# Transposes placed between the products of the next half unit, and the retention's projection moved ahead of the attention gate

## What is computed

```
h = rmsnorm(x, norm1_g) * (1.0 + scale1) + shift1
q_r, k_r, v_r, g_r, q_d, k_d, v_d, gates = split_projection(h @ w_in)
gate_r, gate_d = jnp.split(jax.nn.sigmoid(gates + b_gate), 2, axis=-1)
...
branch_r = (jax.nn.silu(g_r) * y_r) @ w_ret_out        # y_r: normalised output of the retention
branch_d = o_d @ w_diff_out                            # o_d: normalised output of the attention
mix = (gate_r * branch_r + gate_d * branch_d) @ w_o
x = x + gate1 * mix
h2 = rmsnorm(x, norm2_g) * (1.0 + scale2) + shift2
ffn = (jax.nn.silu(h2 @ w_ffn_gate) * (h2 @ w_ffn_up)) @ w_ffn_down
x = x + gate2 * ffn
```

## Time and profile before

| what | value |
|---|---|
| median of three runs | 1375.28 us (1375.09 to 1375.91) |
| the profiled execution | 1375.61 us, of which the span of instructions is 1373.9 us |
| PE busy | 1307.0 us |
| DVE busy | 635.4 us |
| ACT busy | 420.0 us |
| POOL busy | 179.8 us |
| mean granted clock of TensorE | 0.986 |

### The profile page before, as it was taken

How to read it: one execution, slowest core, us unless ns; L and a number is a source line. 1 busy time by engine, 2 the same in 40 slices (tenths; PEclk the granted TensorE clock), 3 DMA queues, 4 the chain that set the end, 5 groups by cost and what they waited for, 6 DMA issues and landing times.

```text
span 1373.9 us, 20027 instructions
## 1 busy us (share of the span) xinstructions
PE 1307.0 (95%) x7974; PEld 1199.1 (87%) x7974; DVE 635.4 (46%) x1001; ACT 420.0 (31%) x642; POOL 179.8 (13%) x189
## 2 busy tenths in 40 slices
PE   4899999999999999998999799899999999999996
PEld 1599887799999999987788798799998999889995
DVE  3734121466657634372898554452224232343245
ACT  5422233344321122213777222242221121212222
POOL 1002000310001011111899200000000000000000
PEclk9999999999999999998999999999999999999998
DMA  9534222143334443452000215111222122221211
GB/s 299 160 103 121 90 64 75 38 154 122 115 130 143 130 121 97 125 188 85 2 2 1 93 62 184 62 62 61 84 69 92 62 69 84 72 82 62 76 46 77
DMA packets 87180, 129.27 MB, mean 94 GB/s; under 512 B 3465, under 2 KB 64386, under 8 KB 86994
## 3 DMA queue, kind: packets, MB, share of 16 engines
q1 hardware_dynamic: 76800, 95.20, 21.3%
q0 software_dynamic: 9104, 32.20, 7.5%
q10 hardware_dynamic: 1218, 1.07, 0.2%
HBM read 117.43 MB, written 4.73 MB: 89 GB/s over the span
## 4 chain that ended last, share of the span: by engine, by line
PE 83%; POOL 6%; DVE 5%; ACT 2%; DMA 2%; issue 1%; DVEq 0%; SPq 0%; ACTq 0%
PE psum L382 50%; PE psum L411 26%; POOL probs L733 3%; POOL probs L739 2%; PE psum L363 1%; DVE ada_acc L1234 1%; DMA x_nat<-in_x_prompt 1%; PE psum L481 1%; PE psum L482 1%; DMA x<-in_x_prompt 1%; PE psum L835 1%; PE psum L833 0%; PE psum L834 0%; DVE hf L524 0%; ACT junk L969 0%
## 5 line engine op out<-in xcount | busy, mean ns | idle before, releaser
L347 DVE TENSOR_TENSOR w_lo<-w_raw,w_hi 128x2048 fp32r<-128x2048 f32 x78 | 178.7, 2291 | 341.5 <-ACT w_hi L342 333.5
L382 PE MATMUL psum<-h_hi,w_lo 128*128 128x320 f32 x1344 | 307.9, 310 | 4.0 <-DVE hf L524 1.4
L382 PE MATMUL psum<-h_lo,w_hi 128*128 128x320 f32 x1344 | 306.8, 309 | 0.0
L382 PE MATMUL psum<-h_hi,w_hi 128*128 128x320 f32 x1344 | 306.8, 309 | 0.0
L382 PEld LDWEIGHTS psum<-h_hi,w_lo 128*128 128x128 f32 x1344 | 225.0, 188 | 5.4 <-issue 4.4
L382 PEld LDWEIGHTS psum<-h_hi,w_hi 128*128 128x128 f32 x1344 | 225.3, 188 | 0.0
L382 PEld LDWEIGHTS psum<-h_lo,w_hi 128*128 128x128 f32 x1344 | 225.1, 188 | 0.0
L342 ACT ACTIVATE w_hi<-w_raw 128x2048 fp32r<-128x2048 f32 x77 | 146.9, 1908 | 209.8 <-PE psum L411 158.5
L411 PE MATMUL psum<-w_lo,h_hi 128*128 128x512 f32 x240 | 93.7, 390 | 0.4 <-ACT mod L1042 0.4
L411 PE MATMUL psum<-w_hi,h_hi 128*128 128x512 f32 x240 | 93.4, 389 | 0.0
L411 PE MATMUL psum<-w_hi,h_lo 128*128 128x512 f32 x240 | 93.4, 389 | 0.0
(11 more groups left out here) (234 smaller groups left out, 1836.3 us busy)
## 6 DMA issues: line engine op xcount, KB each, us to landing
w_raw<-in_w_in SPq DMA_DIRECT2D x32, 1024.0 KB, 5.7
ada_b<-in_w_ada POOLq DMA_DIRECT2D x32, 512.0 KB, 4.0
w_raw<-in_w_ffn_gate SPq DMA_DIRECT2D x11, 1024.0 KB, 5.2
w_raw<-in_w_ffn_up SPq DMA_DIRECT2D x11, 1024.0 KB, 5.2
ada_a<-in_w_ada SPq DMA_DIRECT2D x8, 1024.0 KB, 12.1
w_raw<-in_w_ffn_down SPq DMA_DIRECT2D x8, 1024.0 KB, 4.8
w_raw<-in_w_ret_out SPq DMA_DIRECT2D x4, 1024.0 KB, 4.7
swapped<-qk_d POOLq DMA_DIRECT2D x32, 128.0 KB, 2.5
```

What stands on the lines that cost most here:

```text
L347: dve.tensor_tensor(w_lo[s][:, :, :], w_raw[s][:, :, :], w_hi[s][:, :, :].bitcast(F32), ALU.subtract).then_inc(w_lo_done, 1)
L382: last = pe.matmul(bank(4 * par + 2 * j + h, HALF), w[:, k, cs], x[:, k, h * HALF:(h + 1) * HALF], start=(k == 0 and n == 0), stop=(k == K ...
```

## The change

Three things change. For h, `pe_to_T` keeps its place but now goes round three pairs of banks (2 to 7), so B(k) waits for the readers of B(k-3) instead of B(k-4), and the end waits for tile 5 instead of tile 4. For yg, od and h2 the new `pe_T_and_dense` issues B(0) to B(2), and then P(0), B(3), P(1), B(4), and so on up to B(7) behind P(4); banks 0 and 1 take the products. And ret_out stands ahead of gate_d in every table and on every engine. The core of the diff:

```diff
-          ("gate_r", 4, "act", "act"), ("gate_d", 4, "act", "act"), ("ret_out", 4, "dve", "dve"),
+          ("gate_r", 4, "act", "act"), ("ret_out", 4, "dve", "dve"), ("gate_d", 4, "act", "act"),
...
+        def pe_to_T(pe, which, src):
...
             for k in range(KT):
-                if k >= 4:
-                    wait_read(k - 4)
...
-            wait_read(5 if which == "yg" else 4)
+                if k >= 3:
+                    wait_read(k - 3)
+                tiles_T(pe, which, src, k, 2 + 2 * (k % 3))
+            wait_read(KT - 3)
+
+        def pe_T_and_dense(pe, which, src, name, hi, lo, diagonals=None, by_block=None):
...
+            for k in range(3):
+                block(k)
+            pe_wait_unit(pe, name, 0, 0)
+            for j in range(2):
+                for k in range(KT):
+                    if j == 0:
+                        pe.wait_ge(q["lo"], k + 1)
+                    last = T_products(pe, 0, j, k, hi, lo)
+                    if j == 0 and k + 3 < KT:
+                        block(k + 3)
+                if name in ADA_FIRST and j == 1:
+                    last = pe_ada_sums(pe, name, 0, 0)
+                last.then_inc(mm_done, 1)
+            pe_wait_unit(pe, name, 0, 1)
+            pe_T_unit(pe, name, 0, 1, hi, lo)
+            pe_dense(pe, name, pe_T_unit, hi, lo, first=1)
...
-            pe_to_T(pe, "yg", y_nat)
+            pe_T_and_dense(pe, "yg", y_nat, "ret_out", yg_hi, yg_lo)
             pe_dense(pe, "gate_d", pe_T_unit, h_hi, h_lo)
-            pe_dense(pe, "ret_out", pe_T_unit, yg_hi, yg_lo, split=(n2t["yg"]["lo"], 0))
...
-            pe_to_T(pe, "od", o_nat, by_block=(norm["normo"]["scaled"], od_scaled))
-            pe_dense(pe, "diff_out", pe_T_unit, od_hi, od_lo, split=(n2t["od"]["lo"], 0))
+            pe_T_and_dense(pe, "od", o_nat, "diff_out", od_hi, od_lo, by_block=(norm["normo"]["scaled"], od_scaled))
...
-            pe_to_T(pe, "h2", x1, diag_r)
...
+                if third == 0:
+                    pe_T_and_dense(pe, "h2", x1, "up0", h2_hi, h2_lo, diag_r)
```

More of the change, by code:

```diff
@@ L104 @@
 FIRST, COUNT, READER, BEFORE, START = lay_out_phases()
-ADA_FIRST = {"gate_r": 0, "gate_d": 4, "ret_out": 8, "v_d": 12}
+ADA_FIRST = {"gate_r": 0, "ret_out": 4, "gate_d": 8, "v_d": 12}
 AHEAD = 1
@@ L370, in pe_ada_sums, with T_products @@
             return sums_over_partitions(pe, par, bank(4 * par + 3, 4, HALF))
+        def T_products(pe, par, j, k, hi, lo):
+            cs = slice(j * P, (j + 1) * P)
+            for n, (w, x) in enumerate(((w_lo[par], hi), (w_hi[par], lo), (w_hi[par], hi))):
+                for h in range(2):
+                    last = pe.matmul(bank(4 * par + 2 * j + h, HALF), w[:, k, cs], x[:, k, h * HALF:(h + 1) * HALF],
+                                     start=(k == 0 and n == 0), stop=(k == KT - 1 and n == 2))
+            return last
         def pe_T_unit(pe, name, i, par, hi, lo, split=None):
             for j in range(2):
-                cs = slice(j * P, (j + 1) * P)
                 for k in range(KT):
@@ L379, in pe_T_unit @@
                         pe.wait_ge(split[0], split[1] + k + 1)
[L380 to L384, removed]
+                    last = T_products(pe, par, j, k, hi, lo)
                 if name in ADA_FIRST and j == 1:
@@ L451, in wait_tile, with pe_dense @@
                 engine.wait_ge(mm_done, ready(name, i, 1, 1))
-        def pe_dense(pe, name, unit, hi, lo, **kw):
-            with pe.Fori(0, COUNT[name] // 2) as i:
+        def pe_dense(pe, name, unit, hi, lo, first=0, **kw):
+            with pe.Fori(first, COUNT[name] // 2) as i:
                 for par in range(2):
@@ L457, in pe_dense, with tiles_T @@
                     unit(pe, name, i, par, hi, lo, **kw)
-        def pe_to_T(pe, which, src, diagonals=None, by_block=None):
+        def tiles_T(pe, which, src, k, pair, diagonals=None):
+            for t in range(TILES):
+                out, x = bank(pair + t // 4, P, (t % 4) * P), src[:, t, k * P:(k + 1) * P]
+                last = pe.matmul(out, x, diagonals[:, t, :], start=True, stop=True) if diagonals is not None else \
+                    pe.transpose(out, x, ident[:, :])
+            last.then_inc(n2t[which]["ps"], 1)
@@ L465, in pe_to_T @@
+        def pe_to_T(pe, which, src):
             q = n2t[which]
-            readers = (q["f"], q["f2"]) if which in SHIFTED else (q["lo"],)
             def wait_read(k):
-                for r in readers:
-                    pe.wait_ge(r, k + 1)
+                pe.wait_ge(q["f"], k + 1)
+                pe.wait_ge(q["f2"], k + 1)
             for k in range(KT):
-                if k >= 4:
-                    wait_read(k - 4)
+                if k >= 3:
+                    wait_read(k - 3)
+                tiles_T(pe, which, src, k, 2 + 2 * (k % 3))
+            wait_read(KT - 3)
@@ L476, in pe_to_T, with block @@
+        def pe_T_and_dense(pe, which, src, name, hi, lo, diagonals=None, by_block=None):
+            q = n2t[which]
+            def block(k):
                 if by_block is not None:
                     pe.wait_ge(by_block[k % 2], k // 2 + 1)
[L478 to L482, removed]
@@ L483, in pe_to_T @@
-                last.then_inc(q["ps"], 1)
-            wait_read(5 if which == "yg" else 4)
+                tiles_T(pe, which, src, k, 2 + 2 * (k % 3), diagonals)
+            for k in range(3):
[11 more added lines that the diff above has]
+                last.then_inc(mm_done, 1)
@@ L488, in in_pair @@
+            pe_wait_unit(pe, name, 0, 1)
+            pe_T_unit(pe, name, 0, 1, hi, lo)
+            pe_dense(pe, name, pe_T_unit, hi, lo, first=1)
         def in_pair(k):
-            return psum[:, 2 * (k % 4) * BANK:2 * (k % 4) * BANK + TOK]
+            pair = 2 + 2 * (k % 3)
+            return psum[:, pair * BANK:pair * BANK + TOK]
         def modulated(which, shift, k, c, cs):
@@ L615, in _ @@
             stream("gate_r", columns(w_in, 6144))
+            stream("ret_out", columns(by_tile["w_ret_out"], 0))
             stream("gate_d", columns(w_in, 7168))
-            stream("ret_out", columns(by_tile["w_ret_out"], 0))
             stream("q_d", columns(w_in, 3072))
@@ L705, in _ @@
             pool.wait_ge(r_out, RH * TILES)
-            for name in ("gate_r", "gate_d", "ret_out"):
+            for name in ("gate_r", "ret_out", "gate_d"):
                 with pool.Fori(0, 2) as i:
@@ L847, in _ @@
             pe_dense(pe, "gate_r", pe_T_unit, h_hi, h_lo)
-            pe.wait_ge(freed["act"], START["gate_d"]["act"])
+            pe.wait_ge(freed["act"], START["ret_out"]["act"])
             pe.wait_ge(y_gated, RH)
-            pe_to_T(pe, "yg", y_nat)
+            pe_T_and_dense(pe, "yg", y_nat, "ret_out", yg_hi, yg_lo)
             pe_dense(pe, "gate_d", pe_T_unit, h_hi, h_lo)
-            pe_dense(pe, "ret_out", pe_T_unit, yg_hi, yg_lo, split=(n2t["yg"]["lo"], 0))
             pe_dense(pe, "q_d", pe_T_unit, h_hi, h_lo)
@@ L938, in _ @@
             pe.wait_ge(norm["norm2"]["scaled"], TILES)
-            pe_to_T(pe, "h2", x1, diag_r)
             tiles = 0
             for third in range(3):
-                pe_dense(pe, f"up{third}", pe_T_unit, h2_hi, h2_lo, split=(n2t["h2"]["lo"], 0))
+                if third == 0:
+                    pe_T_and_dense(pe, "h2", x1, "up0", h2_hi, h2_lo, diag_r)
+                else:
+                    pe_dense(pe, f"up{third}", pe_T_unit, h2_hi, h2_lo)
                 kt = COUNT[f"up{third}"]
@@ L1127, in _ @@
             act_to_T(act, "yg", yg_hi, gn_gain)
+            dense("ret_out", lambda i, par: None)
             dense("gate_d", gate("gate_d", gate_d, KT))
-            dense("ret_out", lambda i, par: None)
             dense("q_d", copy_T("q_d", qk_d, 0, DHD ** -0.5))
@@ L1409, in _ @@
             dve_to_T(dve, "yg", yg_hi, yg_lo, gn_gain)
-            dense("gate_d", lambda i, par: None)
             def gated_ret(i, par):
@@ L1422, in _ @@
             dense("ret_out", gated_ret)
+            dense("gate_d", lambda i, par: None)
             ada_partial("v_d", 0, 0)
```

## The result

The changed kernel takes 1389.64 us (median of four runs, 1388.39 to 1391.52). The kernel before took 1375.18 us on the same chip. The ratio is 1.0109, with a 95% interval of 1.0092 to 1.0127, so it is slower by some 15 us. The forecast was 1386.4, with a range of 1382.5 to 1393.

What follows compares the result with a forecast made beforehand. PE was taken to bound the kernel, busy 1307.0 of 1373.9 us, so reordering moves only its idle places and transposes. Terms summed to +11.0 on 1375.3, giving 1386.3, stated as 1386.4, range 1382.5 to 1393 us.

Steps and rivals of the forecast that it cites:

- the ring: At h2: PE and DVE wait for each other in turn, five times, neither covering the other; +11.4 us.
- rival of a lost clock: At h2: clock lost in most of the five turns, total 1389.5 to 1397 us; chance 0.25.
- A turn: At h2: one round of product, block, hf and low part costs 3.94 us, of which PE works 2.0.
- The extra 0.9: At h2: +0.9 us for one short fall of the clock, with full clock for most of the five turns.
- od (-3.6): At od: diff_out's products start at 767.0 instead of 774.23; between -4.3 and -2.8 us, taken as -3.6.
- second slow stretch: At od: the half-clock stretch from 772 to 775 should go, as PE is busier; otherwise -2.8 us.
- h (+1.9, bounds +1.0 and +2.4): At h: products wait for hf of tile 5, +1.0 us, plus +0.9 for a slower clock.
- 3 us at half clock would cost 1.4 more. I take +0.9: At h: PE does little from 57.5 to 62.4, so a half-clock stretch may follow; priced at +0.9 us.
- yg (+0.4): At yg: the 1.32 us stall goes, a 1.7 us wait for ada_acc replaces it; between -0.6 and +1.0 us.
- The sum: Whole kernel: 1.9 + 0.4 - 3.6 + 11.4 + 0.9 = +11.0 us.

Runs made afterwards that it cites:

- e1: Changed kernel with h2's eight blocks back ahead of up0's products, in four pairs of banks; 1378.79 us, ratio 1.0021 to before.
- e2: Changed kernel with, at h2, DVE's low part ahead of the next hf and ACT's high copy ahead of its next shift; 1379.44 us, ratio 1.0035.
- e8: The kernel before, unchanged, run once more for a second profile; 1374.23 us.
- e10: Changed kernel with the modulation columns of ret_out's first unit left out, so part of the modulation vector is wrong; 1386.49 us, ratio 1.0085.
- e7: Changed kernel with three pairs of banks at h but without the end wait for tile 5; 1386.36 us, ratio 1.0087.
- e5: Kernel before with od's blocks between diff_out's products as the only change; 1370.64 us, ratio 0.9975.
- e4: Changed kernel with the modulation columns of ret_out's first unit made on DVE ahead of yg's low parts; 1385.93 us, ratio 1.0081.
- e9: Changed kernel with h and h2 as before (four pairs, blocks ahead), leaving the swap, yg and od; 1373.35 us, ratio 0.9987.
- e6: Kernel before with only the swap of ret_out ahead of gate_d; 1375.54 us, ratio 1.0011.

## Why the forecast held, step by step

The direction, the ring as its cause and its size were right. The total was not hit so closely: 1389.64 lies at the lower edge of the range that was given to the rival of a lost clock (1389.5 to 1397), and that rival's mechanism did not come, since the ring ran at 1.00. What came on top lies at h, in the unit behind yg and at w_o, and part of it was cancelled by chance (below, at "The sum").

**The ring at h2 (forecast +11.4, with +0.9 for the clock).** Right in place, mechanism and size: +11.20 in the stage. A turn took 3.89 us where 3.94 was the sum of its parts, all read from before. P waited 1.64 us in each turn where I had said 1.9, and hf of tile 3 waited 2.42 where I had said up to 2. e1 takes the ring away with the blocks, e2 with the order on DVE alone, and either gets most of the loss back. The extra 0.9 for a fall of the clock inside the ring was not needed; over the five turns PE was busy 11.26 of 19.40 us and was granted 1.00. The ring's bursts of some 2.2 us with waits of 1.64 us kept the full clock, while the stretch at h, 1.55 of 4.80 us busy with single waits of up to 1.46 us, was followed by 0.50. The Trainium skill, in "TensorE: Matmul & The Clock Gate", section "HAM oscillation — how this bites in real kernels", describes a clock that falls again and again where each burst of products is shorter than the wait behind it. The ring is not such a case, its waits being the shorter part, so it does not test that rule.

**od (-3.6).** Right in mechanism, and in size with some luck: -3.88. The products started 3.06 us behind the first transpose instead of 10.36, and the stage took 63.32 to 63.76 in every kernel with the change at od. But the second slow stretch of before, which the sum let go with the change, is not there in e8 either, whose stage took 65.91. So about 2.6 us are the order's, and 1.3 came only because this execution of before had that stretch.

**h (+1.9, bounds +1.0 and +2.4).** Too small: +3.37, beyond the upper bound. The step that failed is "3 us at half clock would cost 1.4 more. I take +0.9". The clock was at 0.50 through 61 to 66, which costs 5.0 / 2 = 2.5 us by itself. The other part, the later start of the products, was right: it is 1.68, and 0.45 of it takes the place of the wait that P(5) had before, which leaves 1.2 where I had 1.0. The two together, 3.7, are a little over what the stage shows. The fall also differs between executions of the same kernel, so a price of it needs more than one: by the means of the five profiles with the wait (67.35) and the six with four pairs (64.72) the term is 2.6, still above the bound.

**yg (+0.4).** Right within its bounds: 0.0. The stall of 1.32 went and a wait of 1.09 for ada_acc came. I had 1.7: DVE's chain ended 0.4 earlier after the first transpose (21.70 instead of 22.1) and the products 0.2 later (20.67 instead of 20.5). e10 shows the gain that was given back, 1.25 (forecast 1.3). Not in the sum was what followed: the next unit took 16.61 instead of 14.97. One stretch of after inside it:

```profile
367.00:369.00 2.00, 2.00 (x10) 2.00 (x9) 1.67 (x1) 0.30 (x1) 0.00 (x0) 0.50 0.54 199
```

In e1 and e2, whose programs are the same up to there, and in e7, which differs only at h, the unit took 15.08. So this cost comes in some executions. The same had stood in before's chain, in gate_r's first unit: a wait ahead of the sums and then 15.7 us for a unit of 14.2. I had the row and did not ask whether a new wait at such a place would repeat it.

**w_o (not in the sum).** +0.98. DVE's split waits there for x1's load from the prompt, and PE for DVE. The chain of after and of e5 (start, length, what):

```profile
834.86 9.74 DMA x<-in_x_prompt
```

```profile
831.71 8.41 DMA x<-in_x_prompt
```

This last piece took 9.7 to 10.1 us in all eight kernels with the blocks between the products at yg (after, e1 to e4, e7, e9, e10: the range is 9.72 to 10.13) and 8.4 to 9.0 in the four runs without (before, e5, e6, e8). e5 excludes that od's part does it. (e1's stage of 62.75 has a slow stretch besides, 847.0 to 850.5 at 0.52.) What about yg, 400 us earlier, goes with it I can't say; it stays open.

**The sum.** By the profiles the forecast had +11.0, and +12.8 came: h +1.5 more, +2.7 between yg and od and +1.0 at w_o that were not in it, against -0.4 at yg, -0.3 at od, -1.1 at h2, and -1.5 ahead of h. The -1.5 is luck: before had a slow stretch ahead of h in this execution, in which the 16 products of ada_a and silu_c took 5.30 us instead of 3.61, and it cancels most of what h cost above the forecast. By the medians the difference is 14.5, and 1.7 of that is not in this pair of profiles; the profiled execution of after, 1388.39 us, is the fastest of its four. Against e8 the span of after is 14.2 us longer.

## What to carry to other kernels

Before putting an engine's work between the pieces of another's, write down what the reader engine does in its own order: where it runs ahead (here two tiles of hf), the block that it wants first now stands behind a product that wants its last result, and two streams that overlapped become one. It costs one sum of a turn from the old trace to see this, and the cure is the reader's order, not the blocks. Place the blocks only where the profile shows PE idle during them (od: -2.6 to -3.9); where they were covered they can only lose, and a stall removed on PE is gained only if the reader's next work, here the columns, is not what PE waits for next. And before a term is priced from one profile, look at the granted clock in its stretch: two profiles of the kernel before differ there by 1.3 us at od, a third of that term.

## What the runs showed of the hardware

- Falls of the granted clock to 0.50 came at one place in some executions and not in others of the same program: at h before had 64.16 and 65.02, at od 67.21 and 65.91, and the unit behind yg took 16.61 or 15.08. Each cost between 0.9 and 2.5 us, as much as a whole term of this change.
- A ring with 1.64 us of waiting in every 3.89 us kept the clock at 1.00.
- The length of one load (the last piece of x, at w_o) was 8.4 to 9.0 us in four kernels and 9.7 to 10.1 in the eight with the change at yg, 400 us earlier; the cause is open.
